# Identity turns behind the modulation passes, and the first two value items interleaved by channel halves

## The reference

```python
sh1, sc1, gt1, sh2, sc2, gt2 = adaln(c, w_ada[i], b_ada[i])                       # silu(c) @ w_ada + b_ada
csh1, csc1, cgt1, csh2, csc2, cgt2 = adaln(c_ctx[None, :], w_ada[i], b_ada[i])
h = modulate(rmsnorm(x, g_norm1[i]), sh1, sc1)                                    # h * (1 + scale) + shift
hc = modulate(rmsnorm(xc, g_norm1[i]), csh1, csc1)
p = h @ w_in[i]                                                                   # 1024 x 2560
pc = hc @ w_in[i]
...
v = p[..., k_end:].reshape(b, n, N_NA_HEADS, HEAD_DIM)
```

## Time and profile before

| | us |
|---|---|
| median of 3 runs | 1286.1 (1283.7 to 1287.41) |
| profiled execution, its own time | 1285.66 |
| its span in the trace | 1283.8 |
| mean granted TensorE clock | 0.985 |
| PE busy | 1221.5 (95%) |
| DVE busy | 936.2 (73%) |
| ACT busy | 709.7 (55%) |

### The profile page before, as it was taken

One profiled execution on the slowest core, in us unless ns is written; L12 is line 12 of the kernel. 1 busy time (PEld: TensorE's weight loads), 2 busy tenths in 40 slices (PEclk: granted clock), 3 DMA queues, 4 the chain that ended last, 5 costly groups with the idle time before them and its releaser, 6 DMA issues. The chain is left out here.

```text
span 1283.8 us, 18718 instructions
## 1 busy us (share of the span) xinstructions
PE 1221.5 (95%) x7310; PEld 1011.4 (79%) x7310; DVE 936.2 (73%) x1107; ACT 709.7 (55%) x837; POOL 253.8 (20%) x205
## 2 busy tenths in 40 slices
PE   4799999999999999999779999999999999999976
PEld 1799888888788788888668888888888888888852
DVE  1755544332678888666669898989999888989848
ACT  3932212111556666332248878787787877778813
POOL 0000000001100010000111542623535265321001
PEclk8899999999999999999999999999999999999988
DMA  9658744435577773610469999999999999999746
GB/s 377 244 189 292 282 150 157 158 114 168 198 227 165 172 167 105 216 56 34 163 230 370 389 389 390 374 391 376 383 388 378 387 375 393 383 378 385 287 178 255
DMA packets 94459, 343.81 MB, mean 268 GB/s; under 512 B 17387, under 2 KB 45731, under 8 KB 66723
## 3 DMA queue, kind: packets, MB, share of 16 engines
q1 hardware_dynamic: 74499, 311.37, 66.2%
q10 hardware_dynamic: 10656, 14.43, 3.8%
q0 software_dynamic: 9216, 16.80, 3.5%
HBM read 313.70 MB, written 39.33 MB: 275 GB/s over the span
## 5 line engine op out<-in xcount | busy, mean ns | idle before, releaser
L2145 DVE TENSOR_TENSOR w_low<-raw,w_high 128x2048 fp32r<-128x2048 f32 x130 | 298.0, 2313 | 28.6 <-ACT w_high L2082 25.8
L2082 ACT ACTIVATE w_high<-raw 128x2048 fp32r<-128x2048 f32 x130 | 244.9, 1911 | 8.6 <-PEq L1384 8.6
L2145 DVE TENSOR_TENSOR w_low<-arena,w_high 128x2048 fp32r<-128x2048 f32 x62 | 141.8, 2290 | 28.1 <-ACT w_high L2082 28.1
L2082 ACT ACTIVATE w_high<-arena 128x2048 fp32r<-128x2048 f32 x62 | 118.2, 1906 | 0.0
L2041 POOL DMA_INDIRECT y_rows<-arena,row x32 | 48.1, 1503 | 324.1 <-ACT arena L2106 322.5
L1992 PE MATMUL p_g<-w_high,x_high 128*128 128x512 f32 x252 | 101.6, 403 | 1.9 <-DVE w_low L2145 1.1
L1992 PE MATMUL p_u<-w_high,x_high 128*128 128x512 f32 x256 | 102.7, 401 | 0.0
L1992 PE MATMUL p_a<-tokens_high,half_high 128*128 128x512 f32 (+1 forms) x272 | 101.8, 374 | 0.1
L1993 PE MATMUL p_a<-tokens_low,half_high 128*128 128x512 f32 (+1 forms) x272 | 100.9, 371 | 0.0
L1994 PE MATMUL p_a<-tokens_high,half_low 128*128 128x512 f32 (+1 forms) x272 | 100.8, 371 | 0.0
L1994 PE MATMUL p_u<-w_high,x_low 128*128 128x512 f32 x256 | 99.9, 390 | 0.0
(11 more groups left out here) (381 smaller groups left out, 2814.5 us busy)
## 6 DMA issues: line engine op xcount, KB each, us to landing
raw<-in_w_gate SPq DMA_DIRECT2D x64, 1024.0 KB, 8.1
raw<-in_w_up SPq DMA_DIRECT2D x64, 1024.0 KB, 7.8
arena<-in_w_down SPq DMA_DIRECT2D x62, 1024.0 KB, 8.3
raw<-in_w_ada SPq DMA_DIRECT2D x24, 1024.0 KB, 7.8
x<-qk_rows SPq DMA_DIRECT2D x6, 1664.0 KB, 8.2
raw<-in_w_chunks SPq DMA_DIRECT2D x9, 1024.0 KB, 5.5
qk_rows<-x SPq DMA_DIRECT2D x18, 512.0 KB, 2.6
yy<-y_rows SPq DMA_DIRECT2D x8, 1024.0 KB, 14.1
```

The costliest lines, as they stand in the source:

```text
L2082: act.activation(x.high[i % SPLITS][:], x.raw[b][:, :], ACT.Copy).then_inc(high_ok, 1)
L2145: dve.tensor_tensor(x.low[i % SPLITS][:], x.raw[home(n, j)][:, :], x.high[i % SPLITS][:], ALU.subtract).then_inc(low_ok, 1)
```

## The change

Twelve identity turns follow each of the modulation passes 3 to 6, and six follow pass 7 (`AWAKE_BLOCK`, `AWAKE_FLAT`; they write `p_v`, which was read long before). The turns at the end of the first block go from 5 to 10. The second block starts with 34 turns into `p_m` (`AWAKE_TOKENS`, a name that no line used before). Items 0 and 1 are computed as first half of 0, first half of 1, second half of 0, second half of 1, and turn(1) comes behind all four. From item 2 on the order is the old one. No other engine's program changes.

```diff
-AWAKE_COLUMNS, AWAKE_TOKENS = 5, 20
+AWAKE_BLOCK, AWAKE_FLAT, AWAKE_COLUMNS, AWAKE_TOKENS = 12, 6, 10, 34
...
                 for k in range(3, KD):
                     modulation(k)
+                    stay_awake(pe, p_v, s.ident[:], AWAKE_BLOCK if k < KD - 1 else AWAKE_FLAT)
...
-                def item(c, i, width, operands):
+                def item(c, i, width, operands, first=0, end=KD):
...
-                    for k in range(KD):
+                    for k in range(first, end):
...
-                    last.then_inc(done, 1)
+                    if end == KD:
+                        last.then_inc(done, 1)
...
-                def value(c, i):
+                def value(c, i, first=0, end=KD):
...
-                for g in range(5):
+                stay_awake(pe, p_m, s.ident[:], AWAKE_TOKENS)
+                for first, end in ((0, KD // 2), (KD // 2, KD)):
+                    for i in range(2):
+                        value(0, i, first, end)
+                turn(1)
+                for g in range(1, 5):
                     value(0, 2 * g)
```

More of the change, by code:

```diff
@@ L846, in part @@
                     return half_chunk(s, x, 2 * c + k // 4)[:, first + n0:first + n1]
-                def value(c, i):
+                def value(c, i, first=0, end=KD):
                     tokens = slice(i * P, (i + 1) * P)
                     item(c, i, 256, lambda k: (s.x_high[:, k, tokens], s.x_low[:, k, tokens],
-                                               part(c, k, s.w_high2, 0, 256), part(c, k, s.w_low2, 0, 256)))
+                                               part(c, k, s.w_high2, 0, 256), part(c, k, s.w_low2, 0, 256)), first, end)
                 def channels(c, i, w, cols):
```

## The result

The changed kernel takes 1290.98 us (median of 13 executions, 1287.61 to 1295.57), the kernel before 1286.2 in the same rounds (13, 1283.7 to 1287.49): **ratio 1.004, 95% interval 1.003 to 1.005**. 1286.0 was forecast, with a range from 1283.0 to 1288.2. The profiled execution has a span of 1289.0 us against 1283.8 [table of before]. Measured once more, the same kernel gave 1289.74, ratio 1.0029 (1.0019 to 1.0039), and the kernel before against itself 1.0003 (0.9993 to 1.0013).

What follows compares the result with a forecast made beforehand. After the start the PE was taken as the bound, so start changes pass on whole. A 1.1 us gain was to be eaten by the clock lost in the gap: 1283.8 + 1.9 + 0.3 = 1286.0 us, range 1283.0 to 1288.2.

Steps and rivals of the forecast that it cites:

- The passes and the barrier: First block: turns hold the clock, pass 7 and `p_c` run faster, the block ends 1.1 us earlier (0.9 to 1.2).
- each period gives back 0.12, and pass 7 starts at 26.95 to 27.0: Modulation passes: a period takes 2.36 us against 2.48 of data, so pass 4's 0.3 us lateness is made up.
- The 34 turns: Start of the second block: 3.7 us from 30.9, to 34.6 or 35; cost 0 to 0.3 us, off the path.
- The interleaving: Items 0 and 1: worth 0 itself, 4.0 us idle behind turn(1) loses the clock, eating the 1.1 us gain: +0.3 us.
- Nothing in the start but the first 50 us of loads: Answer to the no-effect rival (1285.7 us; 0.07 with something far off): only these loads start by something fixed, ahead of use.
- The rival that transposes don't count for the clock: Start of the kernel: turns don't engage the full clock, all runs at half, turn(1) comes 10 us later; 1295.9 us, chance 0.03.

Runs made afterwards that it cites:

- e3: The changed kernel with 30 more identity turns directly behind turn(1), filling the gap before item 2; median 1286.48 us, ratio 1.0001 to the kernel before.
- e5: As e3, with 8 instead of 12 turns behind passes 3 to 6; median 1287.42 us, ratio 1.0008 to the kernel before.
- e6: As e3, without the first block's turns (5 at its end, as before); median 1287.65 us, ratio 1.0008 to the kernel before.
- c3: The changed kernel with 35 tiny transposes ahead of pass 0, 128 added pairs in all; median 1288.56 us, ratio 1.0016 to the kernel before.
- e1: The kernel before with only the interleaved order of items 0 and 1, no added turns; median 1288.63 us, ratio 1.0023.
- c1: The kernel before with 93 tiny 2 x 2 transposes where the PE is idle; median 1289.54 us, ratio 1.0023.
- c4: e6 with 64 tiny transposes ahead of pass 0, 128 added pairs in all; median 1286.44 us, ratio 1.0000 to the kernel before.

## Why the prediction was wrong, step by step

**The passes and the barrier: wrong, 1.1 us.** The clock held, pass 7 and `p_c` got faster by what was forecast (1.04 and 0.56), but the block ended no earlier. The step that failed is "each period gives back 0.12, and pass 7 starts at 26.95 to 27.0". Two things are behind it. A pass with 12 turns takes 2.43 us (18.15 to 20.58), not 2.36, so a period gives back 0.05. The turns among themselves do step by 0.11, as forecast (in e3 30 take 3.44 us, the last of them 0.27: 3.17 for 29 steps); but 12 of them between two passes take 1.46 (19.12 to 20.58), since the steps from pass to turns and back are longer. Pass 3 started 0.7 late (18.15 for 17.44) in this execution, whose clock first rose at 16.0 and not at 13.3, and a late pass stays late. The other is that piece 7 lands about a us later, with the instruction packet, which the forecast did not know of. e5 separates the two: with slack in each period the second alone remains, and the barrier is still where it was. So the second is enough by itself, and e6, without the late piece, has the forecast's gain (1.0 us for 1.1).

**The 34 turns: right.** They took 3.90 us to 35.86 and hid in the wait for `tokens_low`.

**The interleaving: the mechanism right, the size too small.** The gap was 3.84 us for 4.0, nobody profited from the earlier items, the clock was lost in the two profiles of the changed kernel and in c3's. The term was +0.3 after a gain of 1.1 that did not come: item 2 started at 47.99 instead of 46.95, and ran wholly at half clock, both halves in 5.3 us instead of 3.5. It cost 1.7 in this profile. In the other the clock fell only when item 2 had begun (its first half is at full clock, its second at half), and it cost 1.0. c3, with the later stretch restored, is 2.9 us above the kernel before, and e1, the order alone, 2.7 (intervals 0.8 to 3.5 and 1.4 to 4.5): I take that as the price of the start. Why these medians are above what turn(2) shows in the single profiles (1.5 and 0.65) I can't say; the clock falls elsewhere in each execution, and I have one profile of each.

**"Nothing in the start but the first 50 us of loads" starts by something fixed: wrong, some 2 us.** This was the step on which all hung, that what happens behind turn(2) is unchanged; the sum puts nothing for it. The changed kernel has 93 more pairs on the PE; c1, with the pairs alone, is 3.9 us slower (interval 1.4 to 4.6), and c3, with 35 more pairs, takes back 1.2 to 2.4 of the changed kernel's 3.8 to 4.8 us. The terms are thus 2.7 to 2.9 us for the start and about 2 for the number of added pairs. That they add up is no test, since the second is the measured loss less the first; taken from e1 and c1 alone they would be 2.7 and 3.9, more than was measured. Their sizes are known to a us or two. What was shown place by place is 1 us at 270 us in the changed kernel and in c1. The gaps in the attention, 1.16 us at 417 in the changed kernel among them, are tied to the number of added pairs only by the two groups in the table; how they come about is open.

**The rival that transposes don't count for the clock** fell as the rows of before said it would: 27.09 of 29.90 us busy, with turns between the passes and 34 of them in a row, at PEclk 1.00. The Trainium skill ("TensorE: Matmul & The Clock Gate", Part 4) states the opposite; here the measurement decides.

On the packets, the Trainium skill ("Runtime: NRT & Kernel Launch", Instruction fetch mechanics) says that instructions come in blocks of 16 KiB, 256 instructions, through a DMA queue of the sequencer, and that the cost is mostly hidden. The count agrees: 128 pairs are 256 instructions, and with 128 the packets and the later stretch are as before. Nothing in these profiles speaks against "hidden" for the PE itself, but it does not hold for the transfers beside it: up to 1.0 us for one that somebody is waiting for.

No version beat the kernel before. c4 equals it to 0.1%: filling the gap and restoring the count undo the change's loss, and no gain from the better clock at the start can be told.

## What to carry to other kernels

When a change adds or removes instructions on a long engine program, look at where the instruction packets fall afterwards, and run a control with the same number of idle instructions before you believe any difference of a few us. Work that fills a wait on the PE can be worth more than the time it takes: before you move it, ask what the PE does in the place that it leaves, and whether the clock lives through it. Fill a period of a stream to 98% (2.43 of 2.48 us here) and a lateness stays; leave it slack. And name the stretch by which you will judge before you look: the longer one here did not tell the two kernels apart.

## What was not expected of the hardware

- A 16 KB instruction packet takes 1.02 to 1.09 us near 25 us and 0.99 to 1.40 near 266. A 1 MB load under way at that time is late by 1.0 us (27.88 against 26.92 in piece 7), and a series of small DMAs that is being issued takes up to 1.0 us longer (3.44 to 3.49 against 2.45 in ACT's issue).
- 93 tiny transposes that take 2.6 us of idle PE time cost 3.9 us at the end; 128 cost nothing measurable (0.2 of a thousandth, interval -0.8 to 1.3).
- The clock stayed full through and behind a gap of 3.56 us in one execution (e1). With one of 3.84 us it fell in three, twice before the gap ended (changed kernel, c3), once about 1.4 us behind its end. In e3, 30 turns in it kept it.
- A 2 x 2 transpose steps by 0.027 us (60 took 1.64), a 128 x 128 one by 0.11 at full clock within a row of them (30 took 3.44); 12 of them between two passes took 1.46.
